# The two output projections of a two-layer kernel: order of the fold operations, of the weight additions and of the last pair's pieces

## The reference

```
y = h @ w_out                                   # 2048 x 2048
x = layernorm(alpha * x + y) * g + b
x = x + (p @ ple_w) * sigmoid(x @ gate_w)       # 256 x 2048, 2048 x 2048
```

## Time and profile before

| | us |
|---|---|
| median of 3 runs | 2125.99 |
| lowest, highest | 2123.6, 2126.89 |
| the profiled execution, its own time | 2124.34 |
| its span in the profile | 2122.6 |
| TensorE busy | 2089.6 |
| VectorE busy | 1331.1 |
| ScalarE busy | 866.2 |
| GpSimd busy | 449.7 |

### The profile page before, as it was taken

One profiled execution on the slowest core, in us unless ns is written; L12 is line 12 of the kernel. 1 busy time (PEld: TensorE's weight loads), 2 busy tenths in 40 slices (PEclk: granted clock), 3 DMA queues, 4 the chain that ended last, 5 costly groups with the idle time before them and its releaser, 6 DMA issues.

```text
span 2122.6 us, 29880 instructions
## 1 busy us (share of the span) xinstructions
PE 2089.6 (98%) x11050; PEld 1754.3 (83%) x11050; DVE 1331.1 (63%) x2259; ACT 866.2 (41%) x1140; POOL 449.7 (21%) x288
## 2 busy tenths in 40 slices
PE   9999999999999999899999999999999998999999
PEld 7878888888888888798788888888888887897888
DVE  5235575575665666686733498888888965877332
ACT  4225365464464565343622432222323443437221
POOL 0000000000000005420400044445757425204000
PEclk9999999999999999999999999999999999999999
DMA  8332212222212222683333322222222235842331
GB/s 315 139 111 87 80 60 79 79 79 80 77 63 78 79 79 87 197 215 115 109 116 112 129 99 99 99 99 83 96 99 99 99 107 148 237 132 80 130 118 70
DMA packets 46243, 236.65 MB, mean 111 GB/s; under 512 B 5520, under 2 KB 5792, under 8 KB 25424
## 3 DMA queue, kind: packets, MB, share of 16 engines
q1 hardware_dynamic: 33696, 185.61, 25.1%
q0 software_dynamic: 11600, 45.27, 8.0%
q10 hardware_dynamic: 864, 4.72, 0.6%
HBM read 227.19 MB, written 8.39 MB: 111 GB/s over the span
## 4 chain that ended last, share of the span: by engine, by line
PE 90%; DMA 2%; POOL 2%; DVE 2%; ACT 2%; issue 1%; DVEq 0%; ACTq 0%; POOLq 0%
PE G L758 78%; PE X L758 7%; PE T L758 4%; DMA w_raw<-wall_in 2%; PE T L940 1%; POOL tmp L604 1%; POOL tmp L607 1%; DMA chain<-wall_in 1%; ACT w_hi L1244 1%; DVE w_lo L2175 0%; POOL tmp L609 0%; DVE w_lo L1708 0%; DVE folds L2166 0%; ACT w_hi L1497 0%; ACT w_hi L1563 0%
## 5 line engine op out<-in xcount | busy, mean ns | idle before, releaser
L758 PE MATMUL G<-a_hi,w_hi 128*128 128x512 f32 (+1 forms) x2524 | 979.9, 388 | 3.5 <-DVE w_lo L2175 2.8
L758 PE MATMUL G<-a_hi,w_lo 128*128 128x512 f32 (+1 forms) x2524 | 974.1, 386 | 0.0
L758 PE MATMUL G<-a_lo,w_hi 128*128 128x512 f32 (+1 forms) x2524 | 972.3, 386 | 0.0
L1244 ACT ACTIVATE w_hi<-w_raw 128x2048 fp32r<-128x2048 f32 x147 | 281.6, 1916 | 772.2 <-PE G L758 759.7
L1708 DVE TENSOR_TENSOR w_lo<-w_raw,w_hi 128x2048 fp32r<-128x2048 f32 x104 | 242.0, 2327 | 515.6 <-ACT w_hi L1244 512.8
L758 PEld LDWEIGHTS G<-a_hi,w_hi 128*128 128x128 f32 x2524 | 474.2, 188 | 101.7 <-issue 4.6
L758 PEld LDWEIGHTS G<-a_hi,w_lo 128*128 128x128 f32 x2524 | 474.1, 188 | 96.0 <-issue 0.2
L758 PEld LDWEIGHTS G<-a_lo,w_hi 128*128 128x128 f32 x2524 | 474.3, 188 | 94.8 <-issue 0.5
L2404 DVE SCALAR_TENSOR_TENSOR T<-tmp,par,T 128x512 f32<-128x512 f32 x464 | 306.9, 747 | 0.0
L699 POOL TENSOR_TENSOR w_lo<-w_raw,w_hi 128x2048 fp32r<-128x2048 f32 x45 | 207.8, 4618 | 232.0 <-ACT w_hi L1244 232.0
L1497 ACT ACTIVATE w_hi<-w_raw 128x768 fp32r<-128x768 f32 (+1 forms) x86 | 66.2, 782 | 105.0 <-DMA w_raw<-wall_in 40.6
(11 more groups left out here) (338 smaller groups left out, 2289.9 us busy)
## 6 DMA issues: line engine op xcount, KB each, us to landing
w_raw<-wall_in SPq DMA_DIRECT2D x150, 1024.0 KB, 4.8
w_raw<-wall_in SPq DMA_DIRECT2D x38, 384.0 KB, 5.5
w_raw<-wall_in POOLq DMA_DIRECT2D x28, 384.0 KB, 4.9
w_raw<-wall_in SPq DMA_DIRECT2D x36, 256.0 KB, 5.3
chain<-wall_in POOLq DMA_DIRECT2D x16, 384.0 KB, 7.0
other<-wall_in POOLq DMA_DIRECT2D x16, 384.0 KB, 7.5
Y<-w_in POOLq DMA_DIRECT2D x2, 2048.0 KB, 15.3
x_residual<-Y POOLq DMA_DIRECT2D x16, 256.0 KB, 3.7
```

The source lines that it names most:

```text
L758: return pe.matmul(o, l, r, start=start, stop=stop)
L1244: f(w_hi[:, w.slot, :], w_raw[:, w.slot, :], ACT.Copy).then_inc(S("w_hi"), 1)
```

## The change

It does four things.

1. *Folds.* VectorE makes the low parts of folds 0 and 1 ahead of its split of the fourth tile, and those of folds 2 and 3 ahead of the third chunk's emptying. ScalarE makes the high parts of folds 2 and 3 earlier, around piece r1. On GpSimd the load of t3 moves from behind fold 1 to behind fold 2, and the second addition of t3 from behind fold 3 to behind fold 4.
2. *Additions ahead of loads.* In `weight_sums` the addition of b21 comes ahead of the load of t3 for the next pair.
3. *The residual's second quarter* is loaded from ScalarE's queue behind fold 3's high part, not from GpSimd's behind all folds.
4. *The last pair* is multiplied in the order r1, r2, b11, b21, b12, b22, with fixed slots for b12 and b22, and VectorE splits the first PLE tile behind the centring of chunk 14.

```diff
-UNFOLDED = ("r1", "r2", "b11", "b12", "b21", "b22")
+UNFOLDED = ("r1", "r2", "b11", "b21", "b12", "b22")
+UNFOLDED_SLOTS = {"b12": 3, "b22": 2}
...
         def ring_slot(p, name):
-            return piece_number(p, name) % len(RING_AT)
+            n = piece_number(p, name) % len(RING_AT)
+            return UNFOLDED_SLOTS.get(name, n) if p == FOLD_TO else n
...
+            if (p, name) == (FOLD_TO, "b12"):
+                return piece_done(layer, p, "b11")
             return S("piece_done"), layer * (N_PIECES - 1) + n - 3
...
                     if i == 1:
                         add_second(layer, p, "t1", "b12")
+                    if i == 2:
                         pool.wait_ge(S("w_split"), W_OUT[layer] + 2 * p)
                         load_first(layer, p, "t3", "b12")
-                    if i == 3:
+                    if i == 4:
                         add_second(layer, p, "t3", "b22")
-                    if i == 4:
                         pool.wait_ge(*low_made(layer, p, "t1"))
                         add_later(layer, p, "b22")
...
                         load_first(layer, p + 1, "t1", "b11")
-                        pool.wait_ge(*low_made(layer, p, "t3"))
-                        load_first(layer, p + 1, "t3", "b12")
                     pool.wait_ge(*low_made(layer, p, "t2"))
                     add_later(layer, p, "b21")
                     if p + 1 < FOLD_TO:
+                        pool.wait_ge(*low_made(layer, p, "t3"))
+                        load_first(layer, p + 1, "t3", "b12")
                         add_second(layer, p + 1, "t1", "b12")
...
-            residual(0, 1)
             weight_sums(0)
...
-            residual(1, 1)
             weight_sums(1)
...
+                piece_products(layer, p, "b21", one[:, :], *whole(middle, KC), False, True).then_inc(done, 1)
                 piece_products(layer, p, "b12", two[:, :], *whole(PLAIN_K, middle), False, False).then_inc(done, 1)
-                piece_products(layer, p, "b21", one[:, :], *whole(middle, KC), False, True).then_inc(done, 1)
```

ScalarE's list:

```diff
                 fold_high(0)
                 fold_high(1)
                 split(Idx(w + 3))
+                fold_high(2)
                 piece_high(p, "r1")
-                fold_high(2)
+                fold_high(3)
+                part = slice(4 * T, 8 * T)
+                act.dma_start(Y[:, part], (xT, x2_dram)[layer][:, part]).then_inc(S("res_landed1"), 16)
                 piece_high(p, "t1")
-                fold_high(3)
                 fold_high(4)
...
-                for name in UNFOLDED[:4]:
+                for name in ("r1", "r2", "b11", "b21"):
                     piece_high(FOLD_TO, name)
                 out_square(11)
                 out_square(12)
-                piece_high(FOLD_TO, "b21")
+                piece_high(FOLD_TO, "b12")
+                piece_high(FOLD_TO, "b22")
                 out_square(13)
-                piece_high(FOLD_TO, "b22")
```

VectorE's list:

```diff
                 half_sum(0)
+                fold_low(0)
+                fold_low(1)
                 split(Idx(w + 3))
                 half_sum(1)
-                fold_low(0)
-                fold_low(1)
+                fold_low(2)
+                p = FOLD_FROM
+                fold_low(3)
                 half_sum(2)
-                p = FOLD_FROM
                 lows(p, "r1")
-                fold_low(2)
                 lows(p, "t1")
-                fold_low(3)
                 fold_low(4)
...
-                lows(p, "b12")
+                lows(p, "b21")
                 full_add(2 * p - 1)
                 centres(range(12, 14))
                 square_sums(range(11, 13))
-                lows(p, "b21")
+                lows(p, "b12", "b22")
                 square_sums(range(13, 14))
-                lows(p, "b22")
...
                 dve.wait_ge(*drained(bank))
-                split(Idx(w + KC))
                 full_add(14)
                 centres(range(14, 15))
+                split(Idx(w + KC))
                 square_sums(range(14, 15))
```

## The result

| | before | after |
|---|---|---|
| median of the runs, us | 2125.43 | 2108.28 |
| the profiled execution, us | 2124.34 | 2109.98 |
| its span, us | 2122.6 | 2108.3 |

The ratio is 0.992, with a 95% interval of 0.9903 to 0.9937: 17.2 us faster. The prediction said 2107.5 within 2097 to 2118.

What follows compares the result with a forecast made beforehand. TensorE was taken to be busy for all but some 33 us, its waits mainly for low parts of folds and weight pieces. Per layer 4.2 + 1.9 + 3.0 = 9.1, for two layers 18.2 us: 2107.5 us, range 2097 to 2118.

Steps and rivals of the forecast that it cites:

- Edit 1: Folds: low parts of folds 0 and 1 ahead of the split bring the last low part 4.2 us earlier per layer.
- the walk: Layer 0's fold schedule, one engine waiting out the other: last low part near 866.2 instead of 870.42.
- the prediction's own sign of being wrong: At t1 in the folded pair: it is wrong if the clock falls after the single wait of about 1 us.
- the prediction's price of that clock: Behind t1's two long waits: thirteen 512-column matmuls in 4.67 us at mean 0.56, about 2.0 us lost.
- Edit 2: Transfers from the last low part to r1 of pair 4: reordered additions gain net 1.9 us per layer.
- The link that the prediction named: b21's addition in the chain to pair 4: no longer behind t3's load, 2.5 us off its 7.81.
- Edit 3: Residual's second quarter issued earlier, by ScalarE: counted as nothing, since most of the megabyte was already in.
- Edit 4: End of each projection: waits of 0.38, 1.52 and 0.67 us go, with refilling 3.0 us per layer.
- the transfers keep their pace: Rival: pair 4 starts 45.24 us after the last low part as before; 12 to 14 us in all; chance 0.17.
- All waits go: Rival: t4 and both r1 find their pieces in time; 26 us in all, about 2099; chance 0.16.
- Slower: Rival: late t1 low part ahead of fold 5 delays folds and transfers; 10 us late gives 2130; chance 0.03.

Runs made afterwards that it cites:

- split_first: Changed kernel with both engines' split of the fourth tile ahead of fold 1's parts: 2112.56 us, ratio 0.9941 to the kernel before.
- order_back: Changed kernel with the old order in weight_sums, t3's load for the next pair ahead of b21's addition: 2108.09 us, ratio 0.9926 to before.
- folds_only: Kernel before with only the new order of the folds; additions, residual and last pair as before: 2116.59 us, ratio 0.9963.
- tail_only: Kernel before with only the new order of the last pair: 2115.27 us, ratio 0.9959.
- no_tail: Changed kernel with the last pair's new order undone: 2114.96 us, ratio 0.996 to the kernel before.
- folds_back: Changed kernel with the folds' order as before, residual's second quarter still on ScalarE's queue: 2115.7 us, ratio 0.9965 to before.
- res_back: Changed kernel with the residual's second quarter back on GpSimd's queue behind the folds: 2109.85 us, ratio 0.9932 to before.
- light_burst: Changed kernel loading only the first 16 columns of pieces r1, r2 and b11 of pair 3, in both layers: 2104.21 us, ratio 0.9904 to before.
- r1_early: Changed kernel with VectorE's low part of r1 for the next pair made ahead of emptying the finished pair: 2104.42 us, ratio 0.9901 to before.
- chain_first: Changed kernel with t1's addition for the next pair ahead of t3's load: 2129.28 us, ratio 1.002 to before.

## Why the prediction was right, step by step

- **Edit 1, 4.2 us per layer: right, at 3.7 and 3.8.** Each station of the walk is found, with 0.66 us taken off: the low part of fold 0 at 841.7 (said 841.8), the split at 847.6 (848.0), the wait at the fourth tile 1.31 us (1.3), the wait at t1 1.21 us (about 1), the last low part at 866.7 (866.2). No stretch at the lower clock follows the wait at t1. In layer 1, which the prediction did not walk, the stall at the fourth tile is 1.91 us and the clock does fall behind it. That is the prediction's own sign of being wrong, at another place; it cost nothing that can be seen, as TensorE had to wait for the folds anyway and the last low part is 3.8 us earlier there too. The undoing of edit 1 costs 7.4 us by the medians (3.7 in the spans) and brings back the late low part, both waits and the lower clock, so this is shown. In the prediction's price of that clock, the 4.67 us hold twelve products of 512 columns and the end of a shorter one, not thirteen; the 2.0 us stand. That VectorE and GpSimd wait out each other's operations is what the rows and split_first agree on: moved between them, the work came out at the same end. The sentence of the Trainium skill in "SBUF — State Buffer" (SBUF: two separate sides), on the lock held for a whole instruction, fits the 1.70 and 2.65 us.
- **Edit 2, 1.9 us per layer: the step that was mis-sized.** From the last low part to r1 of pair 4 the kernel gained 0.5 and 1.3 us, and then gave 1.0 and 1.4 back in later pairs: together -0.6 us instead of 3.8. The link that the prediction named did get faster, and by more than it said: b21's addition took 4.59 us in layer 0, 3.2 less than before, where 2.5 were taken off. What failed is that the other links were held fixed: b22's addition took 11.06 us instead of 8.19, which ate 2.9 of the 3.2, and t1's addition for pair 4, now issued right behind t3's load, took 10.30 instead of 7.36. Other kernels agree. Over both layers the stretch to r1 of pair 4 takes 90.9, 90.4, 89.0 and 90.4 us with the old order (before, order_back, folds_only, tail_only) and 89.0, 89.9, 88.6, 87.3 and 89.5 with the new one (changed kernel, no_tail, folds_back, res_back, split_first), which is about 1.3 us on average. The waits in pairs 5 and 6 are no sure price of the new order: no_tail, folds_back and split_first have the order and not the waits. By the medians the order is worth nothing (2108.09 with the old one), and one step further in the same direction is 21 us worse.
- **Edit 3, nothing: right** within what these runs can tell (res_back, folds_back). By "DMA: Bandwidth & Descriptors" of the Trainium skill (Issuing engines are not separate DMA queues) another queue brings no bandwidth; res_back, which changes both the queue and the moment, agrees in that no difference can be told.
- **Edit 4, 3.0 us per layer: right in layer 0 (3.2), too small in layer 1 (4.8).** The square sums come 3.61 us behind the first PLE product (said: some 4), and tail_only, with this edit alone, takes all three waits away. The difference between the layers is the 1.6 us of lower clock behind the three waits of before. The prediction looked for the clock's level in the first half of the projection only and took layer 1's end for a copy of layer 0's.
- The sum is partly luck. In the profiled executions edit 1 gave 0.9 us less than said, edit 2 4.4 less and edit 4 2.0 more, and 0.7 were lost ahead of the projections: 14.3 us where 18.2 were forecast. The medians differ by 17.2 us, closer to the forecast than its parts are.
- The rivals: "the transfers keep their pace" came nearest for edit 2: 44.7 and 44.3 us from the last low part to pair 4, where it said 45.24, though by one link faster and another slower; its total is 14.3 us in the profiled executions, about its upper end of 14, and 17.2 in the medians. "All waits go" failed on the chain through t1's addition; light_burst and r1_early show what removes those waits. "Slower" rested on the wait for t1's low part ahead of fold 5: it cost 0.98 us.

What stays open: how much of the 8.9 us that t1's addition still takes is its own cost and how much the two transfers beside it; it was not tried alone. Open too is why b22's addition in pair 3 became slow. In the changed kernel it is issued 1.0 us behind the first of the residual's last two megabytes (11.06 and 10.78 us); before, it was issued 0.5 and 0.8 us ahead of them (8.19 and 5.63), and in order_back 0.7 and 2.6 ahead (7.47 and 4.95). But light_burst, 0.2 and 0.4 us ahead, still has 12.10 and 11.86, and no run moves the residual's issue alone.

## What to carry to other kernels

When two engines block each other's operations, moving one forward is paid by the other: add up the work of both from the new start, and expect part of the gain (here 3.7 us of 8). On a queue written out by hand, look behind a moved load for the next instruction that waits for it and for what is queued behind that one, and price every transfer that will then share the time, not only the one that was brought forward: here 3.2 us won in one addition were 2.9 lost in another, and one more step cost 21 us. A wait that begins where a finished unit is being cleaned up may want only the next unit's first input made before the cleaning, which was worth 3.9 us here for one low part moved.

## What the runs showed of the hardware

- The same three waits (0.38, 1.52, 0.67 us) were followed by the lower clock in layer 1 of before (0.70 over 5.23 us) and in layer 0 of folds_only (0.54 over 7.41 us), and not in the other layer of either kernel nor in either layer of no_tail.
- A single wait of the same length at the same place went both ways. At the fourth tile of layer 1, 1.91 us were followed by the lower clock in the changed kernel (0.50 in the middle, above), and 1.90 us left it up in res_back:

```profile
1753.95:1759.50 5.55, 5.55 (x25) 1.00 0.56 189
```

- An accumulating transfer of 384 KB took from 4.57 to 11.38 us from issue to landing in the changed kernel's chain and up to 14.07 in chain_first; without a burst of 0.9 MB on another queue, 8.87 instead of 11.38 us.
- A GpSimd operation on two SBUF inputs that takes 0.73 us by itself took 1.70 and 2.65 us beside VectorE operations of 1.23 and 2.83 us, which is about what waiting for their ends gives.
